# The fifth couple of the second wide pair, and up weights loaded straight into the ring of low parts

## The chip, the cores and the metric

The kernel runs on one core of a Trainium2 chip. The metric is the device time of one execution in microseconds (us), as the median of several runs. Before the change it is 1890.28 us (three runs, 1889.5 to 1893.02).

## The reference

Two encoder layers on 256 tokens of width 2048, all in 32-bit floats. Each layer is, cut to what matters:

```
h = rms_norm(x) ; proj = h @ w_in                       # 2048 x 4096
attn = three dilated windows, mixed ; pool = multiscale pooling
x = x + rms_norm(concat(attn, pool) @ w_out)            # 2048 x 2048
f = square(relu(rms_norm(x) @ w_up)) @ w_down           # 2048 x 8192, 8192 x 2048
x = x + rms_norm(f)
```

The change touches the last two lines only, the feed-forward part.

## The kernel before

**Products.** Every 32-bit operand is split into a high part (`w_hi`, made by ScalarE, ACT, as a cast) and a low part (`w_lo`, made by VectorE, DVE, as raw minus high). A product is three matmuls: high by high, low by high, high by low. The weights come from HBM in pieces of 512 KB, one per slot. The ring has `RING` = 8 slots of `w_hi` and 8 of `w_lo`. The memory of the `w_lo` slots is also that of `w_raw`: a piece loaded there is overwritten by its own low part.

**Feed-forward part.** The 8192 hidden columns go in four groups of 2048 (g = 0 to 3). A group has four up units (u = 0 to 3, 512 columns each) and then the down product, in two "wide pairs" (q = 0, 1) of 1024 output columns each; group 3 does its second half in another way.

**An up unit** (`turned_unit` on TensorE, PE) goes over the 8 slots in four stretches: bank pair 0 with slots 0 to 3, bank pair 1 with slots 0 to 3, then 0 and 1 again with slots 4 to 7. A slot is given back (`w_used`) in the stretches of bank pair 1, the second and the fourth. The next unit's first stretch needs bank pair 0 back and its second stretch needs bank pair 1 back (`acc_free`). For that, ACT copies half of the bank to `act_f` (`take_half`, line 1386) and DVE adds the other half (`turned_sum`, line 2063). Between these, ACT and DVE prepare the next unit's weights. ACT's order within unit u is: casts of the next unit's slots 0 to 3, `take_half` of bank 0, cast of slot 4, relu, square and cast of bank 0 (lines 1393, 1395, 1401), casts of slots 5 and 6, `take_half` of bank 1, cast of slot 7, the same three for bank 1. Every engine executes its program in this written order.

**Where the weights land.** The up weights go to `raw`, four buffers of 512 KB (line 479). A buffer is free once DVE has made the low part from it (`lo_made`), so a load runs ahead of the slot in the ring. The down weights go to `raw` too if they belong to a "couple", and otherwise straight to `w_raw` (line 524), where the load first waits until PE has given the slot back.

**Couples.** In a wide pair, two pieces of k by two halves of tokens and columns make eight products. For a couple, seven products of sums and differences take their place (`seven`, lines 961 to 963). `SEVEN_AT` says which of the 16 pieces of a wide pair begin a couple: five couples in pair 0, four in pair 1. A couple costs DVE more: a difference in place (`weight_third`, line 2161), two sums (`weight_sums`, lines 2175 and 2180) and the low part of the sums (`sums_lo`, line 2187), beside the two low parts (`two_lo`, line 2199). Four of the seven products use `acc_pair`; four banks of `shared` collect the others over a q = 1 and the next q = 0. `wide_sums` (line 2088) adds the banks of a finished wide pair to `acc` and gives them back. In the last group `combine` (line 2237 and others) adds the shared sums.

Of the kernel before, what the change touches and what calls it, by code (L numbers as in the profile page):

```python
# [45 lines left out]
P = 128  # L46
D = 2048
# [12 lines left out]
CH = 512  # L60
# [79 lines left out]
SEVEN_AT = ((0, 4, 6, 10, 12), (0, 4, 8, 12))  # L140
# [37 lines left out]

def count_loads():

    couples, plain, totals = {}, {}, {}
    for l in range(DEPTH):
        for g in range(FF_GROUPS):
            for q in range(2 if g < FF_GROUPS - 1 else 1):
# [8 lines left out]
    return couples, plain  # L193


COUPLE_LOADS, PLAIN_LOADS = count_loads()


def pair_at(g, q):

    return (q + g + 1) % 2
# [35 lines left out]
def build(nc, x_in, positions, g_mix_pre, w_in, g_attn_out, w_pool, pool_scale, g_pool_out,  # L237
# [222 lines left out]
    with nc.Block() as block:  # L460
# [3 lines left out]
        def _(sp):  # L464
# [32 lines left out]

            def load_wide(l, g, pairs, hu):

                def rows(q, i):  # L500
                    src = w_down[ld(l, 1), ld(g * D + K_ORDER[q][i] * P, P),
                                 ld(pair_at(g, q) * 2 * CH, 2 * CH)]
                    return src.rearrange("a p c -> p (a c)")
# [4 lines left out]
                for q, i in load_order(pairs):  # L508
                    if i in SEVEN_AT[q]:
                        n = SEVEN_AT[q].index(i)  # L510
                        raw_pair = t_buffer(q, n)
# [4 lines left out]
                        else:  # L516
                            sp.wait_ge(lo_made, lows(0, 2 * before) + 2)
                        for m in range(2):
                            sp.dma_start(raw[:, 2 * raw_pair + m, :], rows(q, i + m)
                                         ).then_inc(couple_loaded[2 * raw_pair + m], 16)  # L520
                        continue
                    for m in range(2):
                        sp.wait_ge(w_used, (hu + q * PAIR_HALVES) * PAIRS + i + m + 1)
                        sp.dma_start(w_raw[:, (i + m) % RING, :], rows(q, i + m)
                                     ).then_inc(plain_loaded[(i + m) % RING], 16)
                for p in range(RAW):
                    sp.sem_inc(raw_loaded[p], 16 * PAIR_HALVES * pairs)
                if not PLAIN_LAST[pairs - 1]:
                    sp.wait_ge(lo_made, lows(pairs, 0))
# [553 lines left out]
        def _(act):  # L1083
# [124 lines left out]
            for l in range(DEPTH):  # L1208
# [263 lines left out]
                def turned_unit(g, u, hu):  # L1472
                    split_hi(hu + 2, 0, (0, 1))
                    if (u - 1, 1) in SEVEN_UNIT:
                        s_rest(g, SEVEN_UNIT.index((u - 1, 1)))
                    split_hi(hu + 2, 0, (2, 3))
                    take_half(g, u, 0)
                    split_hi(hu + 3, 1, (0,))
# [1134 lines left out]
```

## Time and profile before

| | |
|---|---|
| median of three runs | 1890.28 us |
| the profiled execution | 1891.74 us, of which the traced span 1889.6 us |
| PE busy | 1873.1 us, 99% |
| DVE busy | 1532.2 us, 81% |
| ACT busy | 1138.8 us, 60% |
| granted TensorE clock | 0.999 |
| read from HBM | 384.62 MB, 208 GB/s over the span |

PE is busy nearly all the time: what can move the end is the number of matmuls and the few places where PE waits. The busy times of DVE and ACT are sums over the span and say nothing of how early each piece of their work is done; for that one reads a stretch of the timeline. A matmul's record (0.38 us) is longer than the distance to the next one, since they are pipelined; the cost of one is the distance between starts.

### The profile page before, as it was taken

To read this page: it belongs to the slowest core of one execution; us is meant where nothing else is said; L and a number is where in the kernel's file an instruction comes from. 1 tells how busy PE (TensorE), PEld (TensorE's weight loads), DVE (VectorE), ACT (ScalarE), POOL (GpSimd) and SP (SyncE) were. 2 spreads that over 40 slices of the span, in tenths; PEclk is the share of its full clock that TensorE was granted. 3 is DMA by queue.
4 is the path that set the end of the run, shared out by engine and by line. 5 is a ranking of instruction groups with operands and counts; after the bars stand their busy time and mean duration, and the time that the engine had idled before them with its cause. 6 is when DMAs were issued, how large, how long until landed. Compare 5 with 4: busy or idle time off the path is not lost.

```text
span 1889.6 us, 27309 instructions
## 1 busy us (share of the span) xinstructions
PE 1873.1 (99%) x9926; PEld 1665.7 (88%) x9926; DVE 1532.2 (81%) x1877; ACT 1138.8 (60%) x1517; POOL 117.7 (6%) x166
## 2 busy tenths in 40 slices
PE   9999999999999999999999999999999999999998
PEld 7988988888988998898888888889889889889987
DVE  6886657898799789799877757688977997897897
ACT  6455656775666566575564556567656656656653
POOL 3920010000000000000000001100000000000000
PEclk9999999999999999999999999999999999999999
DMA  8665366766656756766676544576766657567664
GB/s 290 200 220 182 112 201 210 251 210 221 215 173 216 234 179 217 239 212 205 255 230 222 194 167 134 167 262 195 255 213 198 212 191 233 187 214 242 233 209 162
DMA packets 170642, 395.11 MB, mean 209 GB/s; under 512 B 12224, under 2 KB 14384, under 8 KB 168496
## 3 DMA queue, kind: packets, MB, share of 16 engines
q1 hardware_dynamic: 167904, 377.58, 60.8%
q10 hardware_dynamic: 2640, 16.27, 2.2%
q8 instruction: 56, 0.92, 0.2%
q14 instruction: 42, 0.34, 0.1%
HBM read 384.62 MB, written 9.18 MB: 208 GB/s over the span
## 4 chain that ended last, share of the span: by engine, by line
PE 81%; DVE 11%; DMA 3%; issue 3%; ACT 2%; ACTq 0%; POOL 0%; DVEq 0%; POOLq 0%; SPq 0%
PE acc_pair L662 22%; PE acc_pair L667 12%; PE acc_pair L628 8%; PE acc_pair L629 8%; PE acc_pair L630 8%; PE acc_pair L961 5%; PE acc_pair L962 5%; PE acc_pair L963 5%; DVE w_lo L2199 3%; DVE w_lo L1594 2%; PE shared L963 2%; PE shared L961 2%; PE shared L962 2%; DMA w_raw<-in_w_down 2%; DVE t_sum L2180 1%
## 5 line engine op out<-in xcount | busy, mean ns | idle before, releaser
L1594 DVE TENSOR_TENSOR w_lo<-raw,w_hi 128x1024 fp32r<-128x1024 f32 x463 | 564.7, 1239 | 148.7 <-ACT w_hi L1089 142.5
L1089 ACT CAST w_hi<-raw 128x1024 fp32r<-128x1024 f32 x463 | 480.3, 1051 | 282.7 <-DMA raw<-in_w_up 106.6
L662 PE MATMUL acc_pair<-h_both,w_hi 128*128 128x512 f32 x2176 | 560.4, 380 | 1.5 <-DVE act_f L2063 1.3
L662 PEld LDWEIGHTS acc_pair<-h_both,w_hi 128*128 128x128 f32 x2176 | 371.0, 190 | 32.1 <-DVE act_f L2063 1.5
L667 PEld LDWEIGHTS acc_pair<-h_both,w_lo 128*128 128x128 f32 x2176 | 327.3, 190 | 29.2
L667 PE MATMUL acc_pair<-h_both,w_lo 128*128 128x256 f32 x2176 | 330.5, 274 | 0.0
L1423 ACT CAST w_hi<-raw 128x1024 fp32r<-128x1024 f32 x128 | 127.6, 1045 | 121.4 <-DVE raw L2161 121.4
L628 PE MATMUL acc_pair<-w_hi,h_both 128*128 128x512 f32 x444 | 170.4, 384 | 1.4 <-DVE w_lo L1594 1.2
L961 PE MATMUL acc_pair<-w_hi,f_hi 128*128 128x512 f32 x448 | 170.2, 380 | 0.8 <-DVE acc L2088 0.7
L962 PE MATMUL acc_pair<-w_lo,f_hi 128*128 128x512 f32 x448 | 169.8, 379 | 0.0
L963 PE MATMUL acc_pair<-w_hi,f_lo 128*128 128x512 f32 x448 | 169.8, 379 | 0.0
L629 PE MATMUL acc_pair<-w_lo,h_both 128*128 128x512 f32 x444 | 168.3, 379 | 0.0
L630 PE MATMUL acc_pair<-w_hi,h_both 128*128 128x512 f32 x444 | 168.3, 379 | 0.0
L2199 DVE TENSOR_TENSOR w_lo<-raw,w_hi 128x1024 fp32r<-128x1024 f32 x128 | 150.6, 1218 | 0.0
L628 PE MATMUL acc_pair<-w_hi,f_hi 128*128 128x512 f32 x384 | 148.2, 386 | 1.3 <-DVE acc L2088 1.3
L629 PE MATMUL acc_pair<-w_lo,f_hi 128*128 128x512 f32 x384 | 145.5, 379 | 0.0
L630 PE MATMUL acc_pair<-w_hi,f_lo 128*128 128x512 f32 x384 | 145.5, 379 | 0.0
L2199 DVE TENSOR_TENSOR w_lo<-w_raw,w_hi 128x1024 fp32r<-128x1024 f32 x96 | 114.3, 1221 | 21.2 <-ACT w_hi L1423 20.9
L1423 ACT CAST w_hi<-w_raw 128x1024 fp32r<-128x1024 f32 x96 | 98.2, 1048 | 45.8 <-DMA w_raw<-in_w_down 44.8
L2187 DVE TENSOR_TENSOR t_lo<-t_sum,t_hi 128x1536 fp32r<-128x1536 f32 x64 | 112.1, 1752 | 0.0
L1469 ACT CAST t_hi<-t_sum 128x1536 fp32r<-128x1536 f32 x64 | 94.4, 1476 | 20.6 <-DVE t_sum L2180 12.3
L2425 POOL TENSOR_TENSOR rstd<-mean_sq,minus_half 128x1 f32<-128x1 f32 (+1 forms) x16 | 13.5, 845 | 1405.2 <-DVE ss_post L1609 1132.4
(253 smaller groups left out, 2742.9 us busy)
## 6 DMA issues: line engine op xcount, KB each, us to landing
raw<-in_w_up SPq DMA_DIRECT2D x256, 512.0 KB, 4.4
raw<-in_w_down SPq DMA_DIRECT2D x144, 512.0 KB, 5.0
raw<-in_w_in SPq DMA_DIRECT2D x128, 512.0 KB, 4.8
w_raw<-in_w_down SPq DMA_DIRECT2D x96, 512.0 KB, 6.4
raw<-in_w_out SPq DMA_DIRECT2D x64, 512.0 KB, 5.4
raw_side<-in_w_down SPq DMA_DIRECT2D x16, 512.0 KB, 8.5
x_kept<-x ACTq DMA_DIRECT2D x4, 1024.0 KB, 5.0
x<-x_kept ACTq DMA_DIRECT2D x4, 1024.0 KB, 5.8
```

The costliest lines, as they stand in the source:

```text
L628: pe.matmul(bank[:, :], xh, wh, start=begin and k == 0, stop=False)
L629: pe.matmul(bank[:, :], xh, wl, start=False, stop=False)
L630: mm = pe.matmul(bank[:, :], xl, wh, start=False, stop=end and k == 1)
L662: pe.matmul(acc_pair[b][:, m, :], w_hi[:, slot, col:col + P], x_both.rearrange("p s (a n) -> p s n a", a=2), start=(slot, k) == (0, 0), st ...
L667: mm = pe.matmul(acc_pair[b][:, m, 0:SEQ], w_lo[:, slot, col:col + P], x_hi.rearrange("p (a n) -> p n a", a=2), start=False, stop=(slot, k ...
L961: pe.matmul(bank, xh, in_turn(wh), start=start, stop=False)
L962: pe.matmul(bank, xh, in_turn(wl), start=False, stop=False)
L963: return pe.matmul(bank, xl, in_turn(wh), start=False, stop=stop)
L1089: act.copy(w_hi[:, half * PAIRS + p, :], raw[:, p, :]).then_inc(hi_made, 1)
L1423: act.copy(w_hi[:, slot, :], src).then_inc(hi_made, 1)
L1594: dve.tensor_tensor(w_lo[:, slot, :], src[:, p, :], w_hi[:, slot, :].bitcast(F32), ALU.subtract).then_inc(lo_made, 1)
L2199: dve.tensor_tensor(w_lo[:, slot, :], src, w_hi[:, slot, :].bitcast(F32), ALU.subtract).then_inc(lo_made, 1)
```

## The change

- `SEVEN_AT[1]` gets a fifth couple, at 14: the last two pieces of each second wide pair (three groups in each of two layers) are done as seven products in place of eight.
- All up units but a layer's first (`direct(g, u)`) are loaded into `w_raw`, that is into the slot itself, and each load waits for `w_used` of that slot. ACT casts from `w_raw` (`up_hi`) in the same places of its order as before, and DVE makes the low part in place (`up_lo`).
- The first two couples of a group are loaded during its second up unit, after that unit's own loads were issued, and no longer after the last up unit's.
- On DVE, in a group's last up unit, `weight_third` and `weight_sums` of the second couple stand ahead of the low parts of pieces 2 and 3 and of `turned_sum` of bank 0; in the second wide pair `wide_sums` stands ahead of the low parts of pieces 2 and 3; in the last group a piece of `combine` stands later.

```diff
-SEVEN_AT = ((0, 4, 6, 10, 12), (0, 4, 8, 12))
+SEVEN_AT = ((0, 4, 6, 10, 12), (0, 4, 8, 12, 14))
...
+def direct(g, u):
+    return u > 0 or g > 0
...
                         if before >= 0:
                             bq = 0 if before < COUPLES[0] else 1
                             sp.wait_ge(lo_made, lows(bq, SEVEN_AT[bq][before - bq * COUPLES[0]]) + 2)
-                        else:
-                            sp.wait_ge(lo_made, lows(0, 2 * before) + 2)
-                        for m in range(2):
-                            sp.dma_start(raw[:, 2 * raw_pair + m, :], rows(q, i + m)
-                                         ).then_inc(couple_loaded[2 * raw_pair + m], 16)
+                            load_couple(l, g, q, n)
                         continue
...
-                with sp.Fori(0, CHUNKS) as u:
-                    load_unit(w_up, l, 0, g * D + u * CH, hu + u * 2)
+                for u in range(CHUNKS):
+                    if not direct(g, u):
+                        load_unit(w_up, l, 0, g * D + u * CH, hu + u * 2)
+                        continue
+                    for slot in range(RING):
+                        sp.wait_ge(w_used, (hu + u * 2) * PAIRS + slot + 1)
+                        src = w_up[ld(l, 1), ld(slot * 2 * P, 2 * P), ld(g * D + u * CH, CH)]
+                        sp.dma_start(w_raw[:, slot, :].rearrange("p (k c) -> p k c", k=2),
+                                     src.rearrange("a (k p) c -> p (a k) c", p=P)
+                                     ).then_inc(plain_loaded[slot], 16)
+                    if u == 1:
+                        free = hu if direct(g, 0) else hu + 2
+                        sp.wait_ge(lo_made, free * PAIRS + RAW)
+                        load_couple(l, g, 0, 0)
+                        load_couple(l, g, 0, 1)
...
+                def up_hi(g, u, half, which=range(PAIRS)):
+                    if not direct(g, u):
+                        split_hi(hu0 + HU_F + g * HU_GROUP + u * 2 + half, half, which)
+                        return
+                    for p in which:
+                        slot = half * PAIRS + p
+                        act.wait_ge(plain_loaded[slot], 16 * UP_LOADS[l, g, u, slot])
+                        act.copy(w_hi[:, slot, :], w_raw[:, slot, :]).then_inc(hi_made, 1)
...
                     take_half(g, u, 0)
-                    split_hi(hu + 3, 1, (0,))
+                    up_hi(g, u + 1, 1, (0,))
                     turned_hi(g, u, 0)
-                    split_hi(hu + 3, 1, (1, 2))
+                    up_hi(g, u + 1, 1, (1, 2))
                     take_half(g, u, 1)
...
                         couple_lo(g, 1, 0)
-                        two_lo(g, 1, 2)
                         if not first:
                             wide_sums(g, q)
+                        two_lo(g, 1, 2)
```

SP's queue at the passage from a group's second wide pair (`in_w_down`) to the next group, before (the four `raw<-in_w_up` rows stand for loop bodies):

```order
L519 DMA raw<-in_w_down 128x1024 [waits lo_made]
L519 DMA raw<-in_w_down 128x1024
L524 DMA w_raw<-in_w_down 128x1024 [waits w_used] x4
L533 UNCONDITIONAL_BRANCH
L533 ISA
L479 ISA [waits lo_made]
L479 DMA raw<-in_w_up 128x2x512
```

And now:

```order
L523 DMA raw<-in_w_down 128x1024 [waits lo_made]
L523 DMA raw<-in_w_down 128x1024
L557 DMA w_raw<-in_w_up 128x2x512 [waits w_used] x16
L523 DMA raw<-in_w_down 128x1024 [waits lo_made]
L523 DMA raw<-in_w_down 128x1024 x3
L557 DMA w_raw<-in_w_up 128x2x512 [waits w_used] x16
```

The sixteen up loads of units 0 and 1 wait for slots that PE gives back; the two first couples' four loads stand between those of unit 1 and those of unit 2.

ACT's program from the relu of bank 0 to that of bank 1 in an up unit, before:

```order
L1395 ACTIVATE act_f<-act_f 128x512 [waits relu_made]
L1401 CAST f_hi<-act_f 128x512 [waits f_ready]
L1089 CAST w_hi<-raw 128x1024 [waits w_used,raw_loaded1]
L1089 CAST w_hi<-raw 128x1024 [waits w_used,raw_loaded2]
L1386 COPY act_f<-acc_pair 128x512 [waits flo_made,w_used]
```

And now:

```order
L1425 ACTIVATE act_f<-act_f 128x512 [waits relu_made]
L1431 CAST f_hi<-act_f 128x512 [waits f_ready]
L1510 CAST w_hi<-w_raw 128x1024 [waits plain_loaded5]
L1510 CAST w_hi<-w_raw 128x1024 [waits plain_loaded6]
L1416 COPY act_f<-acc_pair 128x512 [waits flo_made,w_used]
```

No cast changed its place; the wait for a slot and for a buffer loaded ahead became a wait for a load that itself starts when the slot is given back.

DVE's program in a group's last up unit, between the first couple's low parts (`t_lo_97`) and `turned_sum` of bank 1 (the second `act_f<-acc_pair,act_f`), before:

```order
L2187 TENSOR_TENSOR t_lo_97<-t_sum_95,t_hi_92 128x1536
L2199 TENSOR_TENSOR w_lo<-w_raw,w_hi 128x1024 x2
L2063 TENSOR_TENSOR act_f<-acc_pair,act_f 128x512
L2161 TENSOR_TENSOR raw<-raw 128x512
L2175 TENSOR_TENSOR t_sum_96<-raw 128x512
L2180 TENSOR_TENSOR t_sum_96<-raw,t_sum_96 128x1024
L2080 TENSOR_TENSOR f_lo<-act_f,f_hi 128x512
L2199 TENSOR_TENSOR w_lo<-raw,w_hi 128x1024 x2
L2063 TENSOR_TENSOR act_f<-acc_pair,act_f 128x512
```

And now:

```order
L2227 TENSOR_TENSOR t_lo_97<-t_sum_95,t_hi_92 128x1536
L2201 TENSOR_TENSOR raw<-raw 128x512
L2215 TENSOR_TENSOR t_sum_96<-raw 128x512
L2220 TENSOR_TENSOR t_sum_96<-raw,t_sum_96 128x1024
L2239 TENSOR_TENSOR w_lo<-w_raw,w_hi 128x1024 x2
L2103 TENSOR_TENSOR act_f<-acc_pair,act_f 128x512
L2120 TENSOR_TENSOR f_lo<-act_f,f_hi 128x512
L2239 TENSOR_TENSOR w_lo<-raw,w_hi 128x1024 x2
L2103 TENSOR_TENSOR act_f<-acc_pair,act_f 128x512
```

The three operations on the second couple moved ahead of the low parts of pieces 2 and 3 and of the first `turned_sum`.

## Rows read from the trace of the kernel before

**Rows 1.** The page: busy time of the engines.
```profile
PE 1873.1 (99%) x9926; PEld 1665.7 (88%) x9926; DVE 1532.2 (81%) x1877; ACT 1138.8 (60%) x1517; POOL 117.7 (6%) x166
```
**Rows 2.** Waits of PE: engine, line, releaser: us in total, times, longest.
```profile
PE acc_pair L961 <- DVE act_f L2063: 1.0, 2, 0.6
PE acc_pair L961 <- DVE acc L2088: 0.7, 3, 0.4
```
**Rows 3.** Timeline of PE, two matmuls 56 apart: start us, us, then what.
```profile
559.79 0.38 PE L962 MATMUL shared<-t_lo,s_hi 128*128 128x512 f32 x1
...
571.88 0.38 PE L961 MATMUL acc_pair<-w_hi,f_hi 128*128 128x512 f32 x1
```
**Rows 4.** Timeline of ACT, end of an up unit and last unit.
```profile
516.78 1.06 ACT L1089 CAST w_hi<-raw 128x1024 fp32r<-128x1024 f32 x1 [0.77 <-PE acc_pair L667]
...
533.56 1.04 ACT L1423 CAST w_hi<-w_raw 128x1024 fp32r<-128x1024 f32 x1 [1.68 <-DMA w_raw<-in_w_down]
```
**Rows 5.** Timeline of DVE, the same unit, then the last one.
```profile
522.11 0.69 DVE L2063 TENSOR_TENSOR act_f<-acc_pair,act_f 128x512 f32<-128x512 f32 x1 [0.15 <-ACT act_f L1386]
...
525.59 0.68 DVE L2080 TENSOR_TENSOR f_lo<-act_f,f_hi 128x512 fp32r<-128x512 f32 x1
...
545.13 0.68 DVE L2063 TENSOR_TENSOR act_f<-acc_pair,act_f 128x512 f32<-128x512 f32 x1
```
**Rows 6.** Timeline of PE, last up unit of that group: stretches 1 and 2, slot 2's end.
```profile
520.46 0.60 PE L662 MATMUL acc_pair<-h_both,w_hi 128*128 128x512 f32 x2
...
525.70 0.60 PE L662 MATMUL acc_pair<-h_both,w_hi 128*128 128x512 f32 x2
...
529.63 0.60 PE L662 MATMUL acc_pair<-h_both,w_hi 128*128 128x512 f32 x2
```
**Rows 7.** Timeline of SP, and its loads by line: DMA to landing.
```profile
529.82 0.33 SPq L524 DMA_DIRECT2D w_raw<-in_w_down  x1
...
DMA to landing us min/median/max: 3.6/4.6/10.0
```
**Rows 8.** Timeline of ACT, DVE and PE, layer 0, group 0, end of up unit 1.
```profile
337.54 1.05 ACT L1089 CAST w_hi<-raw 128x1024 fp32r<-128x1024 f32 x1 [3.11 <-DMA raw<-in_w_up]
342.23 0.58 ACT L1386 COPY act_f<-acc_pair 128x512 f32<-128x512 f32 x1
342.84 0.69 DVE L2063 TENSOR_TENSOR act_f<-acc_pair,act_f 128x512 f32<-128x512 f32 x1
343.58 0.48 PE L662 MATMUL acc_pair<-h_both,w_hi 128*128 128x512 f32 x1 [1.33 <-DVE act_f L2063]
```
**Rows 9.** Timeline of PE, first wide pair of that group: start, and seventh product.
```profile
541.42 0.38 PE L961 MATMUL shared<-w_hi,s_hi 128*128 128x512 f32 x1
...
545.87 0.48 PE L961 MATMUL acc_pair<-t_hi,f_hi 128*128 128x512 f32 x1 [0.40 <-DVE act_f L2063]
```
**Rows 10.** Timeline of DVE, end of the second wide pair.
```profile
603.02 0.69 DVE L2161 TENSOR_TENSOR raw<-raw 128x512 f32<-128x512 f32 x1
...
605.68 2.36 DVE L2199 TENSOR_TENSOR w_lo<-raw,w_hi 128x1024 fp32r<-128x1024 f32 x2
607.95 1.75 DVE L2187 TENSOR_TENSOR t_lo<-t_sum,t_hi 128x1536 fp32r<-128x1536 f32 x1
609.62 2.35 DVE L2199 TENSOR_TENSOR w_lo<-w_raw,w_hi 128x1024 fp32r<-128x1024 f32 x2
611.92 1.23 DVE L1594 TENSOR_TENSOR w_lo<-raw,w_hi 128x1024 fp32r<-128x1024 f32 x1
...
618.17 1.41 DVE L2088 SCALAR_TENSOR_TENSOR acc<-acc_pair,rstd,acc 128x512 f32<-128x512 f32 x2 [3.39 <-PE acc_pair L963]
```
**Rows 11.** Timeline of PE: next up unit, and a wait in each last group.
```profile
619.84 0.38 PE L662 MATMUL acc_pair<-h_both,w_hi 128*128 128x512 f32 x1
...
925.38 0.48 PE L628 MATMUL acc_pair<-w_hi,f_hi 128*128 128x512 f32 x1 [0.87 <-DVE acc L2088]
...
1860.42 0.48 PE L628 MATMUL acc_pair<-w_hi,f_hi 128*128 128x512 f32 x1 [0.44 <-DVE acc L2088]
```

More of the change, by code:

```diff
@@ L176, in load_order @@
     return order + held
+def direct(g, u):
+    return u > 0 or g > 0
 def count_loads():
-    couples, plain, totals = {}, {}, {}
+    couples, plain, ups, totals = {}, {}, {}, {}
     for l in range(DEPTH):
         for g in range(FF_GROUPS):
+            for u in range(CHUNKS):
+                for slot in range(RING):
+                    if direct(g, u):
+                        totals[slot] = totals.get(slot, 0) + 1
+                        ups[l, g, u, slot] = totals[slot]
             for q in range(2 if g < FF_GROUPS - 1 else 1):
@@ L192, in count_loads, with direct_halves @@
                     couples[l, g, q, n] = totals[at]
-    return couples, plain
-COUPLE_LOADS, PLAIN_LOADS = count_loads()
+    return couples, plain, ups
+COUPLE_LOADS, PLAIN_LOADS, UP_LOADS = count_loads()
+def direct_halves(g):
+    return 2 * sum(direct(g, u) for u in range(CHUNKS)) if g < FF_GROUPS else 0
 def pair_at(g, q):
@@ L496, in load_post_row, with rows_of, load_couple @@
                 sp.dma_start(post_row[:, :], src).then_inc(post_row_loaded, 16)
+            def rows_of(l, g, q, i):
+                src = w_down[ld(l, 1), ld(g * D + K_ORDER[q][i] * P, P),
+                             ld(pair_at(g, q) * 2 * CH, 2 * CH)]
+                return src.rearrange("a p c -> p (a c)")
+            def load_couple(l, g, q, n):
+                for m in range(2):
+                    at = 2 * t_buffer(q, n) + m
+                    sp.dma_start(raw[:, at, :], rows_of(l, g, q, SEVEN_AT[q][n] + m)
+                                 ).then_inc(couple_loaded[at], 16)
             def load_wide(l, g, pairs, hu):
[L500 to L503, printed above, removed]
                 def lows(q, i):
@@ L2266, in combine, with up_lo @@
                         dve.wait_ge(q_step, base + 8)
+                def up_lo(g, u, half, which=range(PAIRS)):
+                    src = w_raw[:, ld(half * PAIRS, PAIRS), :] if direct(g, u) else raw
+                    split_lo(hu0 + HU_F + g * HU_GROUP + u * 2 + half, half, which, src)
                 def wide_pair(g, q, first, last=False):
@@ L2363, in group @@
                     c = 2
-                    for p in range(PAIRS):
+                    for p in range(PAIRS - 1):
                         combine(0, p)
                         split_lo(hu + HU_GROUP - 2, 0, (p,))
+                    split_lo(hu + HU_GROUP - 2, 0, (PAIRS - 1,))
+                    split_lo(hu + HU_GROUP - 1, 1, (0,), raw_side)
                     narrow_sum(g, c, 0)
-                    split_lo(hu + HU_GROUP - 1, 1, (0, 1), raw_side)
+                    split_lo(hu + HU_GROUP - 1, 1, (1,), raw_side)
+                    combine(0, PAIRS - 1)
                     narrow_sum(g, c, 1)
```

56 lines of the change are left out of this document (28 added, 28 removed).

## The prediction

> **What bounds the kernel now.** I read the page first: PE is busy 99% of the span, DVE 81%, ACT 60% [rows 1]. So the end is set by the number of matmuls, and beside it only by what makes PE wait. The waits of PE come next: they are few and short, and those in the feed-forward part are all on DVE giving back accumulator banks (`act_f` line 2063, `acc` line 2088) [rows 2]. There is next to nothing to win from shorter waits, and everything to lose if a bank comes back late in each of the many repeated units. So the third view is the timeline of one group (layer 0, group 1), read for how early DVE's and ACT's pieces are done before PE wants them.
>
> One matmul of 512 columns costs PE (571.88 - 559.79) / 56 = 0.216 us [rows 3], a product of three 0.648 us.
>
> The order in an up unit that matters: the cast of the next unit's slot 4 stands in ACT's program ahead of `take_half` of bank 1, and this ahead of DVE's `turned_sum`, for which the next unit's second stretch waits. The slot is given back late, near the end of the unit. Today the weights are in `raw` by then and the cast starts at once, at 516.78 [rows 4]; DVE's sum starts at 522.11 and takes 0.69, so it ends at 522.80 [rows 5]; PE wants the bank at 525.70 [rows 6]. The slack is 2.90 us.
>
> **The matmuls.** Each fifth couple turns eight products into seven: 3 matmuls less, in 2 layers x 3 groups, so 18 x 0.216 = **3.9 us less** on PE. Nothing hides this, it comes off the end.
>
> **The loads into the slots.** The number of loads and their bytes are unchanged; when they start is not. A load now waits for PE to give back the slot. Such a load is already in the trace: in the last up unit slot 2 is given back at 529.63 [rows 6], SP issues its load at 529.82 [rows 7], and ACT casts it at 533.56 [rows 4], 3.93 us after the slot came free. Slot 4 comes free two stretches later by the same pattern: a stretch is 525.70 - 520.46 = 5.24, a slot 1.31, so 3 x 5.24 + 1.31 = 17.03 after the unit's start at 499.50 (520.46 less 20.96 for four stretches), that is at 516.53; today's cast starts 0.25 later. It will start 3.93 later: a delay of 3.68, which the slack of 2.90 does not cover. PE waits 0.78 us at the second stretch of the next unit.
>
> That this chain really ends in a wait of PE, the trace shows once: in layer 0, group 0 a load lands late, the cast starts at 337.54, `take_half` at 342.23, DVE's sum at 342.84, and PE resumes at 343.58 after having waited [rows 8], 6.04 us after the cast. With the new load the cast starts when the next unit starts (17.03 + 3.93 = 20.96), and PE wants the bank 5.24 later: 6.04 - 5.24 = 0.80. The two ways agree.
>
> The wait does not heal itself: it stands in front of the second stretch, and from there to the next freed slot 4 and on to the next unit everything keeps its distance. It comes at every passage from an up unit to the next one: three per group, two in group 0, 11 per layer, 22 in all. One of them is rows 8 itself, where the wait is there already; I leave it as it is. 21 x 0.78 = **16.4 us more**. Bounds for one: SP's line has landings between 3.6 and 10.0 us after the issue, 4.6 in the median [rows 7]; slot 4's load is issued alone, well after slot 3's, so I take the lone one. At 3.6 the wait is 0.7; at the median, 1.6; nothing but another order on ACT would make it nought.
>
> The Trainium skill ("DMA: Bandwidth & Descriptors", section "Anatomy of one DMA", a fit that it gives for the gpsimd path) puts a transfer at about 2.0 us plus its bytes at 436 GB/s, which for 512 KB would be an estimate of 3.2 us; the wait would then be about 0.3 and the term about 6. The rows differ from it: 3.74 from issue to cast here, and no load of that line under 3.6; the measurement decides.
>
> **The last up unit of a group.** Two things meet. First, the low part of bank 1 of the unit before comes later: it started 8.81 after the cast of slot 4 (525.59 - 516.78) [rows 4, 5], so now 8.81 after the last unit's start S, and DVE is free at S + 9.4. Second, all of this now stands in front of `turned_sum` of bank 0: third and sums of couple 0 (2.66, from 603.02 to 605.68), its two low parts 2.27, the low part of its sums 1.67 [rows 10], and, moved ahead, third and sums of couple 1 (2.66), then the low parts of pieces 2 and 3 (2.27). Together 11.5: `turned_sum` of bank 0 starts at S + 20.95. The wide pair starts at W = S + 20.96 + 0.78, so this is W - 0.8. ACT then does relu, square, cast and the two casts of couple 1 before `take_half` of bank 1: these five took 342.23 - 337.54 less one cast, 3.74 [rows 8], so `take_half` is at about W + 3.7. The second of couple 1's low parts ends 1.2 later on DVE, at W + 4.95, and only then comes `turned_sum` of bank 1; PE resumes 0.74 after its start (342.84 to 343.58 [rows 8]), at W + 5.7. PE wants this bank at the seventh product, 18 x 0.216 = 3.9 after W. That makes a wait of 1.8 us. Today it is 545.87 - 541.42 - 3.89 = 0.56 in this group [rows 9], and about 1.3 over all eight (two waits of 1.0 together, each counted 0.16 short because records overlap [rows 2]). 8 x 1.8 - 1.3 = **13.1 us more**. Bounds: below, 0 each (a gain of 1.3), if DVE were free as early as today, since the couple is loaded in time and the waits for `raw` go; above, 2.7 each if the piece loads land 1 us later. I take 1.8, since it is the sum of pitches that DVE cannot avoid in that order.
>
> **The fifth couple on DVE.** It adds 2.66 before the low parts of pieces 14 and 15 and 1.67 behind them [rows 10]. DVE works without idling through the wide pair, until 611.92, and then waits for PE at 618.17 with 3.39 idle [rows 10]: that is the cover. Piece 14 is wanted 8 products before 619.84 [rows 11], at 614.66, and will be ready at 611.92 + 2.66 = 614.58, which is just enough. The low parts of the next unit's slots 0 and 1 then end at 611.92 + 4.33 + 2.27 = 618.5, the two sums of bank 0 at 619.85, and PE wants the bank at 619.84 - 0.65 = 619.19 [rows 11]. The moved `wide_sums` gives DVE a little of it back; I take a wait of 0.55. In group 0 ACT does `first_sums` in DVE's place and there is room. 4 x 0.55 = **2.2 more**; bounds 0 and 4 x 2.2, half of all that a couple adds.
>
> **What the other moves win.** `wide_sums` in front of pieces 2 and 3 takes away PE's wait on `acc` at the start of the second pair: 0.7 and three times the overlap of 0.16 [rows 2], **1.2 less**. In the last group the bank's sum comes one `combine` step earlier and one low part later, a net 0.45 each of the waits of 0.87 and 0.44 [rows 11]: **0.9 less**. Loading the couples in the second unit costs nothing that I can find: SP issues them behind unit 1's last load, at the end of unit 0, and the next load, for slot 0 of unit 2, is due some 6.5 later; slots 0 to 3 are wanted two stretches (10.5) after they came free, which even a slow load meets.
>
> **The sum.** -3.9 + 16.4 + 13.1 + 2.2 - 1.2 - 0.9 = +25.7 us. The span goes from 1889.6 to 1915.3 and the profiled execution, 2.1 longer than its span, from 1891.74 to about 1917.4. The median of the runs is 1.5 below the profiled execution: 1890.28 + 25.7 = **1916.0 us**.
>
> The Trainium skill ("Trainium Kernel Development and Optimization", section "Best Practices") advises to double-buffer, so that DMA overlaps with compute. The change takes the buffer of the up weights away; the overlap of the transfer with PE stays, and what is lost is ACT's freedom to cast at once. By that rule too the time goes up; the size comes from the rows above alone.
>
> **Rivals.**
> - *The delay is absorbed.* If ACT and DVE had some order or slack that I do not see, only the gains would be left: -3.9 - 1.2 - 0.9 - 1.3 for the couple that is loaded in time, and up to 1.5 where the ACT queue's own DMAs held the casts of rows 8. That is about -8.8, 1881.5 us. For it: a load's distance to its use by PE stays over 7 us. Against it: rows 8 show the in-order chain end in a wait. Chance 0.09.
> - *Only the up units wait.* DVE catches up in the last up unit, so its term is -1.3 and not +13.1: +11.3, 1901.6 us. For it: DVE no longer waits there for the couple, since it is loaded early. Against it: the 11.5 us of work in a row. Chance 0.24.
> - *Contention.* The four couples' loads, those of `x_kept` and the bursts of four put slot 4's load at the median of 4.6: 0.9 more in 22 places and as much in the last units, 1890.3 + 25.7 + 27 = 1943 us. For it: 4.6 is the median of all loads; against it, slot 4's load is issued 6.5 us after slot 3's (a stretch and a slot). Chance 0.07.
> - *DVE alone.* No wait in the up units, but the fifth couple is exposed by half of its 4.3 us in six places: -3.9 + 13 - 2 = +7, 1897 us. For it: DVE has no idle time in the pair. Against it: 3.39 idle behind it. Chance 0.06.
>
> The forecast has 0.54. Slower than before are the forecast and three rivals, with a little of the first rival's mass near nought: slower 0.89, within 0.2% (3.8 us, about what a measurement of this kernel can tell) 0.04, faster 0.07. The range of 8 in 10 takes in the rival of the up units alone and stops short of contention: 1898 to 1929.
>
> **What would show each step.** PE's records should be 18 fewer, at the same 0.216. In the up units, the cast of slot 4 (now `w_hi<-w_raw`) should start as the next unit starts, with "<-DMA w_raw<-in_w_up" before it, and PE should wait on `act_f` at the second stretch, 22 times, 0.8 each; an up unit would last 21.7 and not 20.96. At the seventh product of a group's first pair PE waits 1.8; if it waits under 0.6 there, that step is wrong. If the cast of slot 4 waits and PE does not, the whole argument is.

## The result, and the profile after

| | before | after |
|---|---|---|
| median, same chip | 1890.46 us (4 runs) | 1936.72 us (4 runs, 1935.51 to 1938.72) |
| ratio, 95% interval | | 1.0244 [1.0232, 1.0256] |
| traced span | 1889.6 us | 1933.4 us |
| granted TensorE clock, mean | 0.999 | 0.995 |

The change makes the kernel 46.3 us slower, where 25.7 were forecast; the direction was right, and the time lies above the range. The page's busy row of after, against [rows 1]:

```profile
PE 1882.7 (97%) x9908; PEld 1670.1 (86%) x9908; DVE 1556.0 (80%) x1901; ACT 1146.1 (59%) x1523; POOL 117.7 (6%) x166
```

The 18 matmuls are gone (9926 to 9908), and yet PE is busy 9.6 us longer. That is no proof of a lower clock: in experiment 8 PE is busy for 1876.2 us with as few matmuls and no stretch at a lower clock, since a record (0.38 us) is longer than the distance to the next one (0.216) and each wait lets the rest of it count. The clock is read below, from its own column. The waits of after (engine, line, releaser: us in total, times, longest), against [rows 2]:

```profile
PE acc_pair L692 <- DVE act_f L2103: 21.7, 22, 5.1
PE acc_pair L991 <- DVE act_f L2103: 14.7, 8, 2.4
PE acc_pair L692 <- DVE acc L2128: 2.0, 4, 0.6
ACT w_hi L1510 <- DMA w_raw<-in_w_up: 227.0, 129, 7.8
```

Line 692 is the up unit's matmul and 991 the first of a product of three. ACT's casts of up weights stand and wait for a transfer 129 times. PE's two new waits are the two that the prediction named, 22 at passages and 8 at seventh products. Of the 22, 20 stand at the second stretch of a unit, as forecast; the two longest, 5.1 and 4.3 us, stand at the first stretch of group 0's third unit, which the prediction did not have.

**A passage in an ordinary group.** Timelines of ACT, DVE and PE in after, layer 0, group 1, around the start of its third up unit at 509.84 (start us, us, what, idle before and its releaser):

```profile
509.64 1.04 ACT L1510 CAST w_hi<-w_raw 128x1024 fp32r<-128x1024 f32 x1 [3.10 <-DMA w_raw<-in_w_up]
514.33 0.57 ACT L1416 COPY act_f<-acc_pair 128x512 f32<-128x512 f32 x1
514.94 0.69 DVE L2103 TENSOR_TENSOR act_f<-acc_pair,act_f 128x512 f32<-128x512 f32 x1
515.68 1.13 PE L692 MATMUL acc_pair<-h_both,w_hi 128*128 128x512 f32 x4 [0.44 <-DVE act_f L2103]
```

The cast of slot 4 starts 0.20 before the next unit, `take_half` 4.7 later, the sum 0.6 after that, and PE resumes 0.74 after the sum's start: the chain of [rows 8], link by link. PE wanted the bank at 509.84 + 5.24 = 515.08; it is 0.60 late.

**A seventh product.** In the same group the first wide pair starts at 553.09. DVE and PE in after, against [rows 9]:

```profile
552.13 0.68 DVE L2103 TENSOR_TENSOR act_f<-acc_pair,act_f 128x512 f32<-128x512 f32 x1
...
555.77 2.36 DVE L2239 TENSOR_TENSOR w_lo<-raw,w_hi 128x1024 fp32r<-128x1024 f32 x2 [0.19 <-ACT w_hi L1453]
558.05 0.68 DVE L2103 TENSOR_TENSOR act_f<-acc_pair,act_f 128x512 f32<-128x512 f32 x1
...
558.79 0.48 PE L991 MATMUL acc_pair<-t_hi,f_hi 128*128 128x512 f32 x1 [1.65 <-DVE act_f L2103]
```

PE resumes 5.70 after the pair's start. That is the forecast's W + 5.7, and it recurs in all six groups 1 to 3 (5.69 to 5.71). The steps on the way agree too: the first sum starts 0.96 before the pair where 0.8 was forecast, the second low part ends 5.04 after it where 4.95 was.

**Group 0, which the forecast passed over.** The slots are loaded there while the four pieces of the first couples and ACT's copies of `x` and two tables to HBM are on their way. The windows of before and of after (us of the window; busy us of each engine; granted clock, DMA share, GB/s):

```profile
325.00:332.00 7.00, 7.00 (x44) 6.41 (x43) 4.39 (x13) 3.08 (x5) 0.00 (x0) 1.00 0.72 299
332.00:342.50 10.50, 10.14 (x62) 8.99 (x60) 8.36 (x12) 7.33 (x11) 0.00 (x0) 1.00 0.92 304
```

```profile
325.00:332.00 7.00, 7.00 (x45) 6.44 (x45) 5.11 (x14) 2.61 (x4) 0.00 (x0) 1.00 1.04 400
332.00:342.50 10.50, 5.45 (x35) 4.83 (x34) 5.10 (x6) 4.11 (x7) 0.00 (x0) 0.96 1.02 412
341.70:348.50 6.80, 6.01 (x18) 5.20 (x19) 6.35 (x11) 6.74 (x10) 0.00 (x0) 0.50 0.29 111
```

All DMA engines are busy (share 1.0) at 400 to 412 GB/s. The couples' loads take 7.9 to 10.3 us from issue to landing, the slots' loads 7.0 to 11.8 (in group 1, from 500 to 548, they take 4.4 in the median). What follows, on ACT, DVE and PE of after:

```profile
338.83 1.04 ACT L1510 CAST w_hi<-w_raw 128x1024 fp32r<-128x1024 f32 x1 [3.43 <-DMA w_raw<-in_w_up]
339.78 0.58 ACT L1416 COPY act_f<-acc_pair 128x512 f32<-128x512 f32 x1
...
339.91 1.23 DVE L1634 TENSOR_TENSOR w_lo<-w_raw,w_hi 128x1024 fp32r<-128x1024 f32 x1 [3.25 <-ACT w_hi L1510]
...
341.65 0.68 DVE L2103 TENSOR_TENSOR act_f<-acc_pair,act_f 128x512 f32<-128x512 f32 x1
...
342.49 2.07 PE L692 MATMUL acc_pair<-h_both,w_hi 128*128 128x512 f32 x4 [5.05 <-DVE act_f L2103]
```

Slot 3, not slot 4, is late here. Bank 0's `take_half` stands behind its cast on ACT, and `turned_sum` of bank 0 behind its low part on DVE: from the cast to PE's restart it is 342.49 - 338.83 = 3.66 us. The load was issued at 326.99 and PE wanted bank 0 at the next unit's start, at 337.44, so the load had about 6.8 us to land without harm. It took 11.8. PE waits 5.05 us, and then runs four matmuls in 2.07 us in place of 1.03: the last window shows a granted clock of 0.50, the lower of its two levels (1.2 GHz). The trace has that level for 6.8 us from 341.66 on, of which the first 0.8 still lie in the wait. The same happens for 3.4 us at 1300.8 and at 1352.0, behind waits of 4.3 and 2.4 us. Before, no stretch at the lower level lies ahead of the end.

Put together from the starts of the units in both traces (an up unit was 20.96 long):

| place | forecast | measured |
|---|---|---|
| up units, groups 1 to 3 (18 passages) | +14.0 | +16.5 (0.92 each) |
| up units, group 0 | +2.3 | +14.0 |
| first wide pairs | +13.1 | +16.1 |
| second wide pairs (couple and moved sums) | -2.9 | -2.9 |
| ends of the layers (`combine`) | -0.9 | -1.1 |
| the rest | 0 | +1.2 |
| sum | +25.6 | +43.8 |

The first wide pairs hold 14.2 of later seventh products and 1.9 of the lower clock. The traces are 43.8 apart and the medians 46.3, since the profiled execution is the fastest of the four.

### The profile page after: what moved, and what is told of

Its sections match the earlier page's. It is cut to its first block, busy times and chain, and to the rows that moved or that the text cites. A ratio compares the mean times of both kernels' runs of the same rounds, so it can differ in the third digit from the quotient of the medians.

```text
span 1933.4 us, 26253 instructions
## 1 busy us (share of the span) xinstructions
PE 1882.7 (97%) x9908; PEld 1670.1 (86%) x9908; DVE 1556.0 (80%) x1901; ACT 1146.1 (59%) x1523; POOL 117.7 (6%) x166
## 4 chain that ended last, share of the span: by engine, by line
PE 63%; DVE 20%; ACT 7%; DMA 6%; issue 4%; POOL 0%; DVEq 0%; ACTq 0%; POOLq 0%
PE acc_pair L692 14%; PE acc_pair L658 8%; PE acc_pair L660 8%; PE acc_pair L659 8%; PE acc_pair L697 7%; DVE w_lo L2239 6%; DMA w_raw<-in_w_up 5%; PE acc_pair L991 4%; PE acc_pair L992 3%; PE acc_pair L993 3%; DVE w_lo L1634 3%; ACT w_hi L1510 2%; DVE t_sum L2220 2%; DVE t_lo L2227 2%; PE shared L992 2%
## 5 line engine op out<-in xcount | busy, mean ns | idle before, releaser
L692 PE MATMUL acc_pair<-h_both,w_hi 128*128 128x512 f32 x2176 | 566.4, 383 | 23.8 <-DVE act_f L2103 21.7
L692 PEld LDWEIGHTS acc_pair<-h_both,w_hi 128*128 128x128 f32 x2176 | 373.2, 191 | 60.0 <-DVE act_f L2103 16.1
L1634 DVE TENSOR_TENSOR w_lo<-w_raw,w_hi 128x1024 fp32r<-128x1024 f32 x240 | 289.6, 1222 | 152.8 <-ACT w_hi L1510 151.3
L1510 ACT CAST w_hi<-w_raw 128x1024 fp32r<-128x1024 f32 x240 | 246.9, 1047 | 227.2 <-DMA w_raw<-in_w_up 227.0
L1634 DVE TENSOR_TENSOR w_lo<-raw,w_hi 128x1024 fp32r<-128x1024 f32 x223 | 275.4, 1258 | 74.0 <-ACT w_hi L1119 69.9
L1119 ACT CAST w_hi<-raw 128x1024 fp32r<-128x1024 f32 x223 | 231.9, 1051 | 142.3 <-PE acc_pair L660 63.7
L1453 ACT CAST w_hi<-raw 128x1024 fp32r<-128x1024 f32 x140 | 139.5, 1045 | 120.1 <-DVE raw L2201 120.1
L2239 DVE TENSOR_TENSOR w_lo<-raw,w_hi 128x1024 fp32r<-128x1024 f32 x140 | 164.8, 1219 | 2.6 <-ACT w_hi L1453 2.6
L991 PE MATMUL acc_pair<-w_hi,f_hi 128*128 128x512 f32 x406 | 154.6, 381 | 0.0
L992 PE MATMUL acc_pair<-w_lo,f_hi 128*128 128x512 f32 x406 | 154.4, 380 | 0.0
L993 PE MATMUL acc_pair<-w_hi,f_lo 128*128 128x512 f32 x406 | 154.4, 380 | 0.0
L658 PE MATMUL acc_pair<-w_hi,f_hi 128*128 128x512 f32 x384 | 148.2, 386 | 0.4 <-DVE acc L2128 0.4
L659 PE MATMUL acc_pair<-w_lo,f_hi 128*128 128x512 f32 x384 | 145.5, 379 | 0.0
L660 PE MATMUL acc_pair<-w_hi,f_lo 128*128 128x512 f32 x384 | 145.5, 379 | 0.0
L2227 DVE TENSOR_TENSOR t_lo<-t_sum,t_hi 128x1536 fp32r<-128x1536 f32 x70 | 122.6, 1752 | 0.0
L1499 ACT CAST t_hi<-t_sum 128x1536 fp32r<-128x1536 f32 x70 | 103.4, 1477 | 30.1 <-DVE t_sum L2220 21.9
L1453 ACT CAST w_hi<-w_raw 128x1024 fp32r<-128x1024 f32 x84 | 86.2, 1048 | 28.3 <-DMA w_raw<-in_w_down 26.9
```

Of the source, the lines that this page charges most:

```text
L658: pe.matmul(bank[:, :], xh, wh, start=begin and k == 0, stop=False)
L659: pe.matmul(bank[:, :], xh, wl, start=False, stop=False)
L660: mm = pe.matmul(bank[:, :], xl, wh, start=False, stop=end and k == 1)
L692: pe.matmul(acc_pair[b][:, m, :], w_hi[:, slot, col:col + P], x_both.rearrange("p s (a n) -> p s n a", a=2), start=(slot, k) == (0, 0), st ...
L991: pe.matmul(bank, xh, in_turn(wh), start=start, stop=False)
L992: pe.matmul(bank, xh, in_turn(wl), start=False, stop=False)
```

## The experiments

All are ratios to runs of the kernel before on the same chip. "Changed" is the kernel after, at 1936.72 us. A time against another kernel's is known to 3 to 4 us, by the two intervals. The diffs are cut to their main lines; three dots stand for what is left out.

**1. The fifth couple alone, in the kernel before.**

```diff
-SEVEN_AT = ((0, 4, 6, 10, 12), (0, 4, 8, 12))
+SEVEN_AT = ((0, 4, 6, 10, 12), (0, 4, 8, 12, 14))
```

> The kernel before with the fifth couple of the second wide pair alone; up weights still go through raw, no order is touched. Theory (the loss comes from where the up weights land and from the order on VectorE, not from the couple): -3.9 us for 18 matmuls, and a wait of 0.5 to 1.5 us behind four to six of the second pairs, because raw is given back 2.7 us later there: 1887 to 1895 us. Rival (the couple's extra work on VectorE is what costs): it would show a large part of the 46 us here, 1905 us or more.

Measured 1928.52 us, 1.0189 [1.0175, 1.0203]. My theory missed by 33 us. The time lies where the rival had it, but for another reason than DVE's extra work, as experiment 2 shows. With a couple at the end of the pair, a wait of SP comes into force by itself (`if not PLAIN_LAST`): all low parts of the pair must be made before the next group's first loads. (The changed kernel has this wait no more.) Its row among the waits of SP, then SP and PE at the end of layer 0's group 0:

```profile
SPq L533 <- DVE w_lo L2199: 85.2, 6, 14.2
...
451.49 2.32 SPq L479 DMA_DIRECT2D raw<-in_w_up  x4
...
460.35 2.07 PE L662 MATMUL acc_pair<-h_both,w_hi 128*128 128x512 f32 x4 [2.71 <-DVE acc L2120]
```

The four loads go out together at 451.49, the low parts that stand ahead of `wide_sums` on DVE come late, PE waits 2.71 for a bank, and then runs at half clock (2.07 for four). Six such stretches make 30.7 us at the lower level. Of these 6.3 still lie in the waits, where they cost nothing; half of the other 24.4, about 12 us, is lost.

**2. The same without that wait** (each buffer's own wait stays).

```diff
-                if not PLAIN_LAST[pairs - 1]:
-                    sp.wait_ge(lo_made, lows(pairs, 0))
```

> The fifth couple alone (1928.52) without the one wait that comes with it, in which SyncE stands until every low part of the pair is made before it loads the next group's first unit; each raw slot's own wait stays. Theory (the couple's place at the end of the pair holds the raw buffer itself, the extra wait adds little): 1918 to 1929. Rival (it is the extra wait that delays all four first loads, and with the slots' own waits they come in time): 1889 to 1903.

Measured 1891.2 us, 1.0001 [0.9992, 1.0010]: the rival is right, 37 us hang on one wait. SP and PE at the same place:

```profile
443.91 7.90 SPq L479 DMA_DIRECT2D raw<-in_w_up  x4
...
457.33 1.03 PE L660 MATMUL acc_pair<-h_both,w_hi 128*128 128x512 f32 x4
```

The first load starts 7.6 us earlier, and PE goes on without a wait at full clock. The couple itself costs nothing, and gains nothing that the time shows.

**3. Changed, with both halves taken before slots 4 to 7 are cast** (ACT; DVE's low parts follow).

```diff
                     take_half(g, u, 0)
-                    up_hi(g, u + 1, 1, (0,))
                     turned_hi(g, u, 0)
-                    up_hi(g, u + 1, 1, (1, 2))
                     take_half(g, u, 1)
...
+                    up_hi(g, u + 1, 1, (0, 1))
                     turned_hi(g, u, 1)
+                    up_hi(g, u + 1, 1, (2, 3))
```

> The changed kernel with another order in the up units: on ScalarE and VectorE both halves of a finished unit are taken before the next unit's slots 4 to 7 are cast. The loads are the same. Theory (a cast that waits for its load stands in front of the second half): the waits of TensorE at the second stretch go, 18 of about 0.9 us in groups 1 to 3 and about 3 to 4 us in group 0, so about 19 us less, 1914 to 1919 us. The wait at the end of unit 1 of group 0 (first half late) and that in the first wide pair stay. Rival (the loads themselves are too slow for the ring): TensorE then waits for w_lo and not for act_f, and the time stays within 5 us of 1936.7.

Measured 1919.13 us, 1.0145 [1.0130, 1.0161], 17.6 less than changed, at the upper end of the theory. The waits at line 692 fall from 22 to 6:

```profile
PE acc_pair L991 <- DVE act_f L2102: 14.2, 8, 2.0
PE acc_pair L692 <- DVE act_f L2102: 11.9, 6, 5.3
```

Groups 1 to 3 have 3.9 of their 16.5 us left, group 0 13.1 of its 14.0. So the passages are ACT's order behind a late load; group 0 is something else.

**4. Changed, with group 0's couples loaded in its third unit.**

```diff
-                    if u == 1:
+                    if u == (2 if g == 0 else 1):
```

> The changed kernel, but in group 0 of each layer the first two couples are loaded behind unit 2's weights and not behind unit 1's. Theory (in group 0 the couples' 2 MB, the weights and ScalarE's copies of x to HBM, 2 MB, want the DMA engines at the same time): the two waits of 5.1 and 4.3 us at the end of unit 1 fall to under 1, and with them the two stretches at half clock behind them (10.2 us at half clock, 5.1 us lost): 1921 to 1927 us. Rival (the wait comes from the loads into the slots alone): no more than 3 us less.

Measured 1929.72 us, 1.0208 [1.0192, 1.0223]: 7.0 less, where the theory had 10 to 16 and the rival at most 3. Both stretches at half clock behind these waits are gone (the one at layer 1's seventh product stays), and the second up units are 1.6 and 2.3 longer than before in place of 4.95 and 4.5. So the waits did not fall under 1 (1.5 and 2.1 are left), and the couples are a part of group 0's loss, not all of it.

**5. Changed, with VectorE's old order in the last up unit.**

```diff
                         couple_lo(g, 0, 0)
-                        weight_third(g, 0, 1)
-                        weight_sums(g, 0, 1)
                         two_lo(g, 0, 2)
...
                         turned_sum(g, u, 0)
+                        weight_third(g, 0, 1)
+                        weight_sums(g, 0, 1)
```

> The changed kernel with the old order in a group's last up unit: VectorE makes the low parts of pieces 2 and 3 and the sum of the first half before it turns to the second couple. Theory: the wait at the seventh product of a group's first wide pair (1.8 us in six places, 2.5 in two, 16 in all, and one stretch of 3.4 us at half clock behind it) falls to under 0.3 each: 14 to 18 us less, 1919 to 1923 us. Rival (that wait only passes on the lateness of the unit before): it stays over 1 us, and the time within 6 us of 1936.7.

Measured 1917.12 us, 1.0138 [1.0122, 1.0153]: 19.6 less, more than I expected. The row of line 991 is gone from PE's waits, the seventh product starts 3.89 to 3.99 after the pair in all eight groups, and the half clock behind that wait in layer 1's group 0 does not occur (the two behind group 0's second up units do, 6.8 us each). So the wait at the seventh product is made by the order of DVE's work. In the trace this order also takes 1.1 us off the second wide pairs and 0.6 off the layers' ends.

**6. The three edits at once.**

> The changed kernel (1936.72) with the three edits at once: both halves taken before slots 4 to 7 are cast, group 0's couples one up unit later, and the old VectorE order in the last up unit. Theory: the loss sits in three places that do not depend on each other, so the gains add: 1936.7 - 17.6 - 7.0 - 19.6 = 1892.5, up to 4 us less gained where one stretch of half clock is counted twice: 1891 to 1897. Rival 1 (the same bytes through one set of slots keep the DMA queues behind, and a place that is freed shows the next late load): 1900 to 1912. Rival 2 (the fifth couple's five saved slots show once the stalls are gone): below 1889.

Measured 1892.37 us, 1.0006 [0.9997, 1.0015]. The three prices add (1892.5), closer than their uncertainty would let one expect: these three places are the whole loss within 3 to 4 us, and with them gone the change makes no difference that can be measured. What is left is 4.8 us in the up units of groups 1 to 3 and 2.4 in group 0, against 4.2 less in the second wide pairs and 2.9 less at the layers' ends.

**7. Changed, with four couples in the second pair.** Edit 1 taken back.

> The changed kernel with four couples in the second wide pair as before, all else as changed. Theory: the couple itself takes 2.9 us off the second wide pairs of the changed kernel (3 per layer) and nothing of the loss hangs on it: 1937 to 1941. Rival 1 (the couple delays the loads behind it and part of the loss is its): 1925 to 1933. Rival 2 (it does nothing either way): 1935.5 to 1937.

Measured 1938.23 us, 1.0249 [1.0235, 1.0263], 1.5 above changed, which is less than the two can be told apart by; the 4 to 12 us of rival 1 are excluded. No such part of the loss is the couple's. The sum of the second wide pairs is 1.9 less than before with four and 2.9 with five.

**8. Changed, with group 0 as before**, through `raw`, and its couples behind unit 3.

```diff
-    return u > 0 or g > 0
+    return g > 0
...
+                        elif g == 0:
+                            sp.wait_ge(lo_made, lows(0, 2 * before) + 2)
+                        if before >= 0 or g == 0:
                             load_couple(l, g, q, n)
```

> The changed kernel with group 0 of each layer as before: its units 1 to 3 through the raw buffer and its first couples loaded after unit 3; groups 1 to 3 as changed. Theory: group 0's part of the loss is units 1 to 3 of both layers in the changed trace, 4.95+1.32+0.77 and 4.52+1.77+0.66 = 14.0 us, and 0.7 us in each first wide pair over the 1.8 of the other groups; the 1.8 us there and all of groups 1 to 3 stay: 1920 to 1923. Rival 1 (only the couples moved ahead hurt group 0, as when they alone were moved): 1928 to 1931. Rival 2 (the slots' wait costs group 0 as much when raw): above 1933.

Measured 1918.04 us, 1.0148 [1.0133, 1.0164]: 18.7 less, a little below my bounds. In the window 332 to 342.5 it moves 326 GB/s and PE does not wait (its wait of before, 1.3 us at 343.58, is still there with 1.0):

```profile
332.00:342.50 10.50, 10.40 (x63) 9.36 (x62) 8.66 (x13) 7.63 (x11) 0.00 (x0) 1.00 0.96 326
```

Two of eight groups carried 18.7 of the 46 us.

**9 and 10. Changed, with ACT's copies issued behind its work of unit 1; then couples and copies both later.**

```diff
-                        for t in range(T):
-                            act.dma_start(x_kept[l, t], x[:, t, :]).then_inc(x_saved, 16)
...
                                 turned_unit(g, u)
+                            if u != 1:
+                                continue
+                            for t in range(T):
+                                act.dma_start(x_kept[l, t], x[:, t, :]).then_inc(x_saved, 16)
...
```

> The changed kernel with ScalarE's copies out (the residual and, in layer 0, two tables, together up to 2.75 MB) issued behind its work of group 0's unit 1 and not ahead of it. Theory (couples, copies and slot loads share the DMA engines in unit 1, so taking away one of the two extra streams gives back about what moving the couples did, 7 us): 1927 to 1932. Rival 1 (the couples alone delay the slots, since they are issued first on the same queue): 1935 to 1937.5. Rival 2 (the copies are the whole of it): 1922 to 1925.

> Both moved: couples loaded one up unit later and the copies issued behind ScalarE's work of unit 1. Theory (unit 1's slot loads are alone in both layers, only the 0.8 to 1.0 us of every passage is left there): 8 to 12 us under the changed kernel, 1924 to 1928.5, below either move alone. Rival (the two streams then meet in unit 2 instead and cost there): 1929 to 1935.

Measured 1929.65 us, 1.0198 [1.0181, 1.0215], and 1933.93 us, 1.0228 [1.0211, 1.0245]. The first is where the theory put it, in part by luck: layer 0's unit 1 is down to 0.3 over before, but now PE waits 4.47 and 2.85 us at the end of unit 2, where unit 3's slot loads meet the copies, and group 0's units are still 11.0 over before against 14.0. The second missed: the two moves do not add, and the rival was right. Its DMA and PE rows:

```profile
344.80:361.00 16.20, 14.39 (x88) 13.02 (x87) 5.26 (x9) 7.84 (x15) 0.00 (x0) 1.00 1.03 412
...
364.95 2.07 PE L692 MATMUL acc_pair<-h_both,w_hi 128*128 128x512 f32 x4 [5.76 <-DVE act_f L2105]
```

With both moved, unit 1 is free of the wait, but now unit 3's slot loads meet the streams: 412 GB/s again, 7.4 to 12.6 us to land, and PE waits 5.76 at the end of unit 2 and falls to half clock. Experiments 4, 9 and 10 try three arrangements, and in each one PE waits in group 0. I put this down to the slot loads, which are due soon after their slot is free (6.8 us for slot 3 above); other places were not tried.

**11. Only the first up unit of groups 1 to 3 into the ring.** That is what the fifth couple wants out of `raw`. Units 1 to 3 go through `raw` as before, couples behind unit 3, DVE's old order in the last unit.

```diff
-    return u > 0 or g > 0
+    return u == 0 and g > 0
...
                     if not direct(g, u):
-                        load_unit(w_up, l, 0, g * D + u * CH, hu + u * 2)
+                        if u == 1 and g > 0:
+                            sp.wait_ge(lo_made, hu * PAIRS + RAW)
+                        load_unit(w_up, l, 0, g * D + u * CH, hu + u * 2,
+                                  2 if u == 1 and g > 0 else 0)
                         continue
```

> The changed kernel with only the first up unit of groups 1 to 3 loaded into the ring of low parts; units 1 to 3 go through the raw buffer as before (unit 1's loads wait until the fifth couple has left it), the first couples are loaded after the last up unit as before, and the last up unit has VectorE's old order. Theory: the fifth couple needs only that first unit out of the raw buffer; the up units have 20.96 us again, group 0 has no second stream of loads, the seventh product is on time, and the second wide pairs keep their 2.9 us: 1885 to 1889, faster than before (1890.5). Rival 1 (the first unit alone costs what it costs in the changed kernel and more, since units 0 and 1 now want loads at once): 1891 to 1897. Rival 2 (the couple costs as it did alone, 1928.5, whatever the first unit's way in): above 1905.

Measured 1886.52 us (9 runs), 0.9979 [0.9969, 0.9989]: 4.1 us faster than before, the best of all. Its busy row, and its longest waits of PE in the feed-forward part:

```profile
PE 1868.5 (99%) x9908; PEld 1663.3 (88%) x9908; DVE 1555.0 (83%) x1901; ACT 1145.7 (61%) x1523; POOL 117.5 (6%) x166
...
PE acc_pair L692 <- DVE acc L2128: 1.6, 4, 0.6
...
PE acc_pair L692 <- DVE act_f L2103: 0.9, 1, 0.9
```

All up units of groups 1 to 3 are back at 20.96 to 21.06, and group 0's are as before (its third keeps its old wait of layer 0, 0.5 shorter). The traces are 6.1 apart: 2.7 are the second wide pairs, 1.7 the layers' ends and 1.2 earlier seventh products. Each of these is too small for the times to show alone.

**12. The same with four couples.**

> The kernel with only the first up unit loaded into the ring (1886.52), with four couples in the second wide pair instead of five: what the fifth couple is worth once nothing else is lost. Theory (18 products less are 3.9 us, of which the second wide pairs' ends give part back): 1887.5 to 1890, so the couple is worth 1 to 3.5 us. Rival 1 (it is worth nothing, the gain is the first unit's and the moved combine's): 1886 to 1887. Rival 2 (all 3.9 us and more): above 1890.2.

Measured 1888.38 us, 0.9987 [0.9978, 0.9996]. Between the ratios of 11 and 12 lie 1.5 us, with an uncertainty of 2.5: the couple's worth is not settled by the time. In the trace the second wide pairs are 0.8 shorter with five, since 3.1 of the 3.9 come back as waits at their ends.

**13. The moved `combine` alone, in the kernel before.**

```diff
-                    for p in range(PAIRS):
+                    for p in range(PAIRS - 1):
                         combine(0, p)
                         split_lo(hu + HU_GROUP - 2, 0, (p,))
...
+                    combine(0, PAIRS - 1)
                     narrow_sum(g, c, 1)
```

> The kernel before with only the last of the combine steps moved behind the first narrow sum and the low parts that stood behind it. Theory: it takes 0.9 to 1.0 us off each layer's end, as the lengths from the last group's first wide pair on show (-1.2 and -1.5 with the move, -0.2 and -0.5 without): 1888 to 1889.5. Rival (the shorter end comes from the first wide pair and not from the move): 1890 to 1891.

Measured 1890.32 us, 1.0000 [0.9991, 1.0009]: inconclusive. The lengths from the last group's first wide pair on are 1.4 and 1.1 shorter, of which 0.3 and 0.6 are an earlier seventh product. The trace leaves 1.1 and 0.6 for the move, more than forecast together; the time can't show so little.

**14. All three, with group 0 through `raw`.**

> Groups 1 to 3 loaded as in the changed kernel, group 0 as before, both halves taken before slots 4 to 7 are cast, the last up unit's old order. Theory: against the version with all three edits (1892.37) group 0's second up unit loses its remaining 1.7 and 2.2 us, while groups 1 to 3 keep 0.5 to 1.1 us in each second up unit: 1888 to 1890. Rival (the order with both halves first costs where the raw buffer feeds it, since a cast then waits behind them): 1892 to 1896.

Measured 1891.71 us, 1.0001 [0.9992, 1.0010]; my theory missed by 2. Group 0's second unit is free as expected, but its seventh product now comes 5.7 after the pair, 1.7 late in each layer:

```profile
PE acc_pair L994 <- DVE act_f L2105: 3.2, 2, 1.7
```

The trace has the link: with the low parts of slots 6 and 7 behind both halves, `raw` is given back later, the first couple's load is issued 15.7 us ahead of the pair in place of 19.4 before, and DVE's work on it starts 10.0 us ahead in place of 13.9. The rest of the chain was not tested by a run.

## Why the prediction was right or wrong

- *What bounds the kernel, and the chain*: right. PE's matmul count, its waits for banks and the lower clock behind the longest of them explain the difference; the link from cast to PE holds in after as in [rows 8].
- *The passages*: right in kind and in number (22, two of them at another stretch than forecast), 0.92 against 0.78 in groups 1 to 3. Slot 4's load was indeed the lone one: 3.40 to 3.83 us to land in these 18 places. From its cast to PE it is 6.05 to 6.14 in 15 of them, as the 6.04 of [rows 8]; in three it is 6.40 to 6.64, since slot 6's load came late too and held the next cast, ahead of `take_half`, by 0.25 to 0.49.
- *The last up unit*: right. 1.8 was forecast, 1.81 measured in groups 1 to 3; in group 0 it was 2.5, and in layer 1 a half clock of 3.4 us cost 1.9 more.
- *The fifth couple and the moved `wide_sums`*: the sum -2.9 was met, by luck. Experiment 7 splits it: without the couple the second wide pairs are already 1.9 shorter, where 1.2 stood, and the couple adds 1.0, where -3.9 + 2.2 = -1.7 stood. Two errors of 0.7 cancel. That the couple needs the direct first unit was nowhere in the prediction; experiments 1 and 2 show that it needs it only against one wait, which costs 37 us.
- *"Loading the couples in the second unit costs nothing that I can find"*: this step failed, and with it the size. I counted when SP would be free to issue the loads, and not who else was using the DMA engines: four couple pieces, four slots and 2.75 MB of ACT's copies in layer 0 (2 MB in layer 1). Experiments 4, 8, 9 and 10 show that it is these streams together: with either of them moved the wait at the end of unit 1 falls, and with group 0's weights through `raw` it is gone. The sentence on slots 0 to 3 failed beside it: it gave their loads 10.5 us, but slot 3's had 6.8, since ACT's and DVE's work on it stands ahead of bank 0; the load took 11.8. The trace of before had the copies' neighbourhood already full (304 GB/s, share 0.92), and [rows 8] lie in it: I read them as a proof of the chain and not as the warning that this place has no room. Group 0's units made 14.0 where 2.3 stood. The rival of contention had the right kind of cause, but spread it over all units; it sits in two of eight groups, and got 0.07.
- *The clock*: not in the prediction. A long wait is paid twice: with three of them PE was at the lower level for 13.7 us, 0.8 of it still in a wait, which costs about 6.4 us, part of the lines above. With what group 0's units (11.7) and the first wide pairs (3.0) made beyond their terms, clock included, the forecast would have been about 1931, above its range too.

The Trainium skill ("DMA: Bandwidth & Descriptors", section "Where 436 GB/s comes from") says that between HBM and SBUF the HBM side binds at about 358 GB/s per core, which it gets as half of a stack's 716, and that 435 is the limit of the ports. In this case one core runs alone, and its trace goes above the first figure: in group 0 the couples' four pieces land from 324.39 to 328.27, one of 512 KB each 1.29 us, which is 405 GB/s, and ACT's first copy out is only issued at 327.47. It stays under the second.

## What to carry to other kernels

A buffer that lets a load run ahead is worth the lateness of every in-order instruction behind the cast that it feeds; before it is taken away, work out that chain for each repeated unit, and check whether the buffer is needed for one unit alone. For every load that is moved, list all transfers on every queue in the same 15 us, not only the queue's own order: by the 1.29 us of a piece above, a stream of 2 MB holds each load behind it for an estimated 5 us. And look in each edit for a wait that switches itself on.

## What the runs showed of the hardware

- With the DMA engines of the core full (share 1.02 to 1.04 in three windows of after and of experiment 10) they moved 400 to 412 GB/s, and layer 0's slot loads of 512 KB took 7 to 12.6 us from issue to landing. Slot 4's lone one took 3.4 to 3.8 at the 18 passages of groups 1 to 3.
- PE's clock fell to its lower level for 3.4 or 6.8 us around the end of long waits, from 2.6 us before it to 0.9 behind it. In the traces of after and of the experiments, all 16 waits of PE of 3.9 to 6.4 us in the feed-forward part went with such a fall, 6 of 14 of 1.87 to 2.85 us, and none of the shorter ones (the longest has 1.77). In experiments 2, 6, 8, 11, 13 and 14, whose waits in that part all were under 1.7, none lies ahead of the end, nor in 12 with one wait of 2.03. What decides between the two lengths stays open.
